# Second attention: the product that finds the row maximum uses 64 array rows, and VectorE makes 2 of 18 low parts

## The reference, cut to what matters

```
def _attend(q, k, v):
    """Bidirectional GQA softmax attention swept over 128-query blocks.
    q (B, L, ATTN_HEADS, HEAD_DIM); k, v (B, Lk, ATTN_KV_HEADS, HEAD_DIM) -> (B, L, ATTN_WIDTH)."""
    ...
    scale = HEAD_DIM ** -0.5

    def one_block(q_blk):
        s = jnp.einsum('bqhgd,bkhd->bhgqk', q_blk, k).astype(jnp.float32) * scale
        p = jax.nn.softmax(s, axis=-1)
        return jnp.einsum('bhgqk,bkhd->bqhgd', p.astype(v.dtype), v)
```

## Time and profile before

| what | us |
|---|---|
| median of three runs | 4641.51 |
| the three runs | 4638.52 to 4641.57 |
| span of the profiled execution | 4644.3 |
| busy in it: PE, DVE, ACT, POOL | 4175.3, 3047.7, 2399.2, 1346.7 |
| this stage, first maximum product to last output | 2332.3 to 3178.6 |
| low parts on POOL (L2241), 576 | 762.2 |
| maxima on DVE (L2384), 384 | 367.1 |
| exponentials and high parts on ACT (L2350, L2352), 576 each | 340.8, 364.2 |

### The profile page before, as it was taken

How to read it: one execution, slowest core, us unless ns; L and a number is a source line. 1 busy time by engine, 2 the same in 40 slices (tenths; PEclk the granted TensorE clock), 3 DMA queues, 4 the chain that set the end, 5 groups by cost and what they waited for, 6 DMA issues and landing times. The chain is left out here.

```text
span 4644.3 us, 62663 instructions
## 1 busy us (share of the span) xinstructions
PE 4175.3 (90%) x22026; PEld 3459.4 (74%) x22026; DVE 3047.7 (66%) x3934; ACT 2399.2 (52%) x3774; POOL 1346.7 (29%) x872
## 2 busy tenths in 40 slices
PE   7999889999886897999889999996499599999985
PEld 5777679898765786888767877785477488888872
DVE  6676555555476775444367676764655699999885
ACT  3434333333311554334378888885422377777763
POOL 0000044444311000000089999993000021212123
PEclk9999989999998998999989999998799699999997
DMA  5343352222286433222250000004433388878957
GB/s 184 128 157 124 136 167 97 85 95 94 93 232 186 160 103 129 64 74 68 64 189 14 14 16 19 14 10 117 161 127 129 140 324 315 341 304 334 382 229 303
DMA packets 368665, 687.98 MB, mean 148 GB/s; under 512 B 71424, under 2 KB 267136, under 8 KB 350592
## 3 DMA queue, kind: packets, MB, share of 16 engines
q1 hardware_dynamic: 339280, 621.71, 38.8%
q10 hardware_dynamic: 15408, 30.81, 2.1%
q0 software_dynamic: 13824, 33.58, 1.9%
HBM read 588.73 MB, written 194.51 MB: 169 GB/s over the span
## 5 line engine op out<-in xcount | busy, mean ns | idle before, releaser
L2241 POOL TENSOR_TENSOR a_PL<-a_PT,a_PH 128x512 fp32r<-128x512 f32 x576 | 762.2, 1346 | 69.0 <-ACT a_PH L2352 67.4
L2384 DVE TENSOR_REDUCE a_part<-a_pA 128x1 f32<-128x1024 f32 (+1 forms) x384 | 367.1, 958 | 243.5 <-PE a_pA L2264 240.5
L3236 POOL DMA_INDIRECT w_XG<-between_h,all_slots x64 | 186.4, 2913 | 742.1 <-PE e_pT L3247 668.0
L2350 ACT ACTIVATE a_PT<-a_pB 128x512 f32<-128x512 f32 x576 | 340.8, 592 | 98.3 <-PE a_pB L2287 96.9
L2352 ACT ACTIVATE a_PH<-a_PT 128x512 fp32r<-128x512 f32 x576 | 364.2, 632 | 18.4
L1044 ACT ACTIVATE a_PT<-a_pT 128x512 f32<-128x512 f32 x128 | 69.5, 595 | 408.5 <-PE a_pT L974 408.5
L886 POOL TENSOR_TENSOR a_QL<-a_RQ,a_QT 128x512 fp32r<-128x512 f32 x16 | 20.6, 1285 | 880.9 <-DVE a_QP L1114 880.9
L1079 DVE TENSOR_REDUCE a_maxima<-a_pS 128x1 f32<-128x512 f32 x256 | 176.5, 690 | 145.6 <-PE a_pS L956 143.1
L988 PE MATMUL a_pO<-a_V,a_PT 128*128 128x128 f32 x2048 | 249.4, 275 | 0.3 <-DVE a_PT L1092 0.3
L988 PEld LDWEIGHTS a_pO<-a_V,a_PT 128*128 128x128 f32 x2048 | 243.4, 192 | 5.9 <-DVE a_PT L1092 0.6
L2225 POOL MEMSET a_QA<- 64x1024 f32 x2 | 1.8, 944 | 846.5 <-POOLq L1822 846.5
(11 more groups left out here) (574 smaller groups left out, 10904.3 us busy)
## 6 DMA issues: line engine op xcount, KB each, us to landing
w_gate<-in_moe_w_gate SPq DMA_DIRECT2D x49, 2048.0 KB, 7.4
w_up<-in_moe_w_up SPq DMA_DIRECT2D x48, 2048.0 KB, 11.6
w_down<-in_moe_w_down SPq DMA_DIRECT2D x47, 2048.0 KB
between_yb<-e_Y SPq DMA_DIRECT2D x46, 512.0 KB, 7.0
a_row_w<-in_w_ada SPq DMA_DIRECT2D x16, 1024.0 KB, 5.3
between_x<-m_X SPq DMA_DIRECT2D x32, 512.0 KB, 3.0
between_yb<-a_zeros SPq DMA_DIRECT2D x31, 512.0 KB, 7.7
between_tv<-p_OV SPq DMA_DIRECT2D x16, 576.0 KB, 2.8
```

Source lines behind the costliest of these rows:

```text
L2241: pool.tensor_tensor(PL[:, t % RING, :], PT[:, t % RING, :], PH[:, t % RING, :].bitcast(F32), ALU.subtract).then_inc(S["p_low"], 1)
L2350: act.activation(PT[:, t % RING, :], pB[t % 2][:], ACT.Exp, scale=scale).then_inc(S["p_ready"], 1)
L2384: dve.tensor_reduce(part[:, h, r % (NG2 // G4):r % (NG2 // G4) + 1], src, AX_X, ALU.max).then_inc(S["maxed"], 1)
```

## The change

The product for the maximum drops the queries' low part, and the two halves of the array get different keys. The first half of a group's keys is multiplied in array rows 0 to 63 with `QA1`'s high part into bank 0 of `pA`, the second half in rows 64 to 127 with `QA2`'s high part (which stands there already) into bank 1. A group of 1024 keys stays two products of 512 columns; a group of 256 becomes two of 128 instead of one of 256. The reduction reads both banks.

The low parts of steps 15 and 17 of every unit are made by VectorE (`low_part_of`) and raise a semaphore of their own; GpSimd leaves them out, so it makes 16 in a unit. The two stand behind `finish(u-1)` and ahead of `split_queries(i+1)`.

```
+    BY_DVE = (KT2 - 3, KT2 - 1)
...
+        def lows_before(t, by_dve):
+
+            u, j = divmod(t, KT2)
+            of_dve = len(BY_DVE) * u + sum(n < j for n in BY_DVE)
+            return of_dve if by_dve else t - of_dve
...
             for t in range(STEPS):
+                if t % KT2 in BY_DVE:
+                    continue
                 pool.wait_ge(S["p_high"], t + 1)
...
                 free(c)
-                for at in range(lo, hi, BANK):
-                    n = min(BANK, hi - at)
-                    mm = pe.matmul(pA[c % 2][:, (at - lo) // BANK, 0:n], QA1[i % 2][:, g * G4 + h, :], KH[g][:, at:at + n], start=True, stop=True)
+                mid, head = (lo + hi) // 2, g * G4 + h
+                pe.matmul(pA[c % 2][:, 0, 0:mid - lo], QA1[i % 2][0:HD, head, :], KH[g][0:HD, lo:mid], start=True, stop=True)
+                mm = pe.matmul(pA[c % 2][:, 1, 0:hi - mid], QA2[i % 2][HD:P, head, :], KH[g][HD:P, mid:hi], start=True, stop=True)
                 mm.then_inc(S["max_ps"], 1)
...
-                pe.wait_ge(S["p_low"], t + 1)
+                if j in BY_DVE:
+                    pe.wait_ge(S["p_low_dve"], lows_before(t, True) + 1)
+                else:
+                    pe.wait_ge(S["p_low"], lows_before(t, False) + 1)
...
-                src = pA[c % 2][:].rearrange("p a b -> p (a b)")[:, 0:hi - lo]
+                src = pA[c % 2][:, :, 0:(hi - lo) // 2]
...
+            def low_part_of(t):
+                dve.wait_ge(S["p_high"], t + 1)
+                dve.tensor_tensor(PL[:, t % RING, :], PT[:, t % RING, :], PH[:, t % RING, :].bitcast(F32), ALU.subtract).then_inc(S["p_low_dve"], 1)
...
                 if u >= 1:
                     finish(u - 1)
+                for j in BY_DVE:
+                    low_part_of(u * KT2 + j)
                 if g == 0 and i + 1 < NT:
                     split_queries(i + 1)
```

More of the change, by code:

```diff
@@ L14 @@
 AX_X = mybir.AxisListType.X
+AX_XY = mybir.AxisListType.XY
 ds = bass.ds
@@ L2184, in attention_2 @@
         names = """v_loaded v_ones k_zeros k_rows k_split k_high q_zeros q_high_act q_high q_split max_ps maxed top_ready row_ps row_ready
-            v_high v_low p_high p_low s_ps p_ready o_ps rec_ready o_ready zeros_ready yb_zeroed""".split()
+            v_high v_low p_high p_low p_low_dve s_ps p_ready o_ps rec_ready o_ready zeros_ready yb_zeroed""".split()
         S = {n: k.sem(n) for n in names}
@@ L2378, in maximum @@
                 c = u * TURNS + r
-                n = (hi - lo) // BANK
-                src = pA[c % 2][:].rearrange("p a b -> p (a b)")[:, 0:hi - lo]
+                src = pA[c % 2][:, :, 0:(hi - lo) // 2]
                 dve.wait_ge(S["max_ps"], u * NG2 + r + 1)
@@ L2383, in maximum @@
                     dve.wait_ge(S["top_ready"], u)
-                dve.tensor_reduce(part[:, h, r % (NG2 // G4):r % (NG2 // G4) + 1], src, AX_X, ALU.max).then_inc(S["maxed"], 1)
+                dve.tensor_reduce(part[:, h, r % (NG2 // G4):r % (NG2 // G4) + 1], src, AX_XY, ALU.max).then_inc(S["maxed"], 1)
             def top_of(u):
```

## The result

The changed kernel takes 4819.58 us (median of four runs, 4818.83 to 4821.39) against 4640.6 of the kernel before: a ratio of 1.0387, with a 95% interval from 1.0374 to 1.0399, so 179 us slower. The forecast was 4673, in a range up to 4740. The direction was right, the size was not: the loss is nearly six times the 31 us of the forecast.

The account below looks back on a forecast made before the run. TensorE was taken as the bound, except where it waits for VectorE's query split. The terms -63.6 + 61 + 3 + 31 gave +31 us, so 4673 us for the median, 0.7% slower, in a range of 4620 to 4740.

Parts of the forecast that it names:

- part 1: Maximum products on TensorE: 64-row pairs run side by side, saving 2.05 us a unit in 31 units, -63.6 us.
- part 2: VectorE's queue: low parts ahead of the query split end it 4.05 us later in 15 even units, +61 us.
- units without a split: Odd units: the first maximum comes after step 17's low part, so TensorE waits 0.2 us, 16 times, +3 us.
- part 3: TensorE behind the longer pause at group 0: the clock drops, 2.1 us each, 15 times, +31 us.
- no cost for the change: TensorE at each group's maximum products: going from 128 rows to 64 and back taken as free; bound 0.32 us a group.
- nearest row: Four turned maxima on TensorE, one array column of 128: 0.11 us each, read as leaving no 0.16 for entry or exit.
- Rival 2: TensorE empties itself at each change between 64 and 128 rows: 0.32 us a group, +120, 4793 us; chance 0.16.
- Rival 3: The two products of a maximum group do not overlap: nothing saved, 63.6 us more, 4737 us; chance 0.12.
- Rival 1: At the query split: short stall, +2.75 us per even unit, clock holds; -22 us, 4619 us; chance 0.14.
- One link: VectorE's low part of step 17, ready at 2736.89, waits for GpSimd's low part and starts at 2737.0.
- no bound: GpSimd loses 64 of 576 low parts; it was not the bound, so nothing is gained from that directly.

Follow-up runs that it names:

- part 1 alone: Changed kernel with only the 64-row products for the maximum, GpSimd keeping all 18 low parts: 4725.27 us, ratio 1.0179 to the kernel before.
- filled against not: Kernel before with only the low parts moved to VectorE, plus 18 unread products in each of 15 pauses: 4698.63 us; without them 4733.0.
- the run with shared rows: Changed kernel with all low parts on GpSimd and both products of a group in array rows 0 to 63: 4809.08 us, ratio 1.0356.
- run with late low parts: Kernel before with low parts of steps 15 and 17 on VectorE, placed behind the query split: 4628.85 us, ratio 0.9972.
- the low parts alone: Kernel before with low parts of steps 15 and 17 on VectorE ahead of the query split, products unchanged: 4733.0 us, ratio 1.0197.

## Why the prediction was wrong

| term | forecast | measured | by |
|---|---|---|---|
| part 1, products in 64 rows | -63.6 | +84.9 | part 1 alone |
| part 2, the split later, even units | +61 | +60 | waits, 76.7 against 16.6 |
| part 2, units without a split | +3 | 0 | 25.07 from unit to unit, as before |
| part 3, clock | +31 | +33 | filled against not |
| sum | +31 | +177 | stage |

**Part 1 is the step that failed, and in it the words "with no cost for the change".** The two products do run side by side (2.4 us a unit against running them one behind the other). The price of going from 128 to 64 rows and back was bounded in the text from nothing to 0.32 us a group by the earlier trace rows, and nothing was taken, by the earlier trace rows. It is 0.40, over the upper bound: 31 x 12 x 0.40 = 149, and -63.6 + 149 = 85, as measured (with the small groups' pair still at 0.06). Each way alone is about 0.2: the bound had only what of a product outlives the next start, 0.16. The weights, which had been loaded beside the product ahead and now are not, were not in that bound.

The earlier trace rows were the wrong nearest row. The turned maxima use one column of the array, and all 128 rows. Their entry and exit cost nothing that the rows show, which says nothing of a change in the rows. The trace of before has no row that bears on it, and then the upper bound deserved as much weight as the lower: with 0.16 a way the sum was 4793, and the chance for it was 0.16 only.

The order of the rivals was wrong for the same reason. Rival 2 has a cost at each change between 64 and 128 rows, and that is what happened, at 0.40 and not 0.32 a group; that TensorE empties itself there, which is the reason it gives, no run shows. Its place in the trace was named rightly (a step of 1.5 to 1.9 us; it is 1.76). Rival 3, no overlap, is refuted by the same start of both products and by the 74 us that the run with shared rows costs. Rival 1, a short stall with the clock kept, is refuted by the pause of 5.09 and the clock of 0.53.

Beside it stood the rule of the Trainium skill ("TensorEngine Tiling (Array Packing)", Key Properties) that a change of the tiling mode drains TensorE. It was given less weight than the earlier trace rows, and it pointed the right way: the loads of the weights that wait for "issue" at exactly the two changes of each group agree with it. What of the 0.40 is the emptying and what the load of weights that no longer hides, no run separates: the timelines give 0.09 ahead of the first product of the new kind and 0.11 behind it, at each change. Why it is these two stays open.

**Part 2 held nearly to the row.** The low part of 17 waits for ScalarE, forecast in the trace of before at 2736.89 against a split that stood finished at 2737.37. The split comes 4.05 later by forecast, and 5.09 - 1.18 = 3.9 by the pauses. The subtraction runs alone, 1.22, as foreseen, with the two copies at 0.69 and 1.65. One link was not there: the low part of 17 was to wait for GpSimd until 2737.0, and it starts 0.03 behind ScalarE's high part. The Trainium skill says of the shared port that whichever of the two engines starts first has it for the whole instruction ("SBUF — State Buffer", Who interferes with whom). The run with late low parts agrees: VectorE's subtraction starts first and takes 1.22, and GpSimd's low part takes 1.72 instead of 1.29. That a subtraction without a wait for GpSimd could turn part 2 into a gain, once it stands behind the split, the forecast did not say, and the expectation for that run missed it.

**Part 3 held.** The forecast took 2.1, midway between the 1.55 and 2.6 of its two rows; the pauses of 5.09 cost 2.2 in the mean. That the middle came so near is luck, the mechanism is not. Behind a pause of 1.08 the clock stayed at 1.00.

**GpSimd** was no bound, as said: with 64 low parts fewer it is busy 669 us instead of 772, and it waits more.

## What to carry to other kernels

Before products are packed into parts of the array, count how often TensorE changes between part and whole: here each way in and out cost 0.40 us, more than the 0.227 that a pair of 512 columns saved, and two such pairs together only broke even. So such products must stand together in longer runs or have a phase of their own, which no run here tried. When work moves to an engine with slack, ask where in its queue it stands and what it waits for there; ahead of a result that another engine needs, two operations of 0.7 us, which had to wait for a third engine, cost 93 us, and behind it the kernel was 10.8 us faster than before. Where no row shows an operation, a row that is like it in another way is no reason to pick an end of the range.

## What the runs showed of the hardware

- Going from products in 128 array rows to products in 64 and back cost TensorE 0.36 to 0.41 us in and out together, with 512 columns and with 128, and with one pair or two pairs of 512 in between. The weights of the first product behind a change were not loaded ahead: in one step the load started 0.31 us behind the product before it, where others start with that product.
- Two products of 512 columns in rows 0 to 63 and 64 to 127 start within 0.01 us of each other. Both in rows 0 to 63 start 0.34 apart.
- Four products with one column of weights and 128 rows between others of 128 rows cost 0.11 us each, and no way in or out could be seen.
- A product of 128 columns costs more than its columns: cutting 256 into two of 128 cost 0.09 us.
- Behind a pause of 5.09 us TensorE ran at the lower clock level for some 4 us in the changed kernel and 5 us with the low parts alone, and 2.2 to 2.4 us were lost each time; filled with products that nothing reads, the same wait left a pause of 1.08, and the clock stayed at 1.00.
- A subtraction of VectorE (64 by 1024) takes 1.22 us where it starts ahead of GpSimd's low part, and 2.21 where one is under way.
